# A decoder layer: compressed attention steps moved ahead of the units, and the first layer norm fed tile by tile

## The reference, cut to what matters

```python
h = layer_norm(x, ln_emb_g, ln_emb_b)                    # x: 512 tokens x 1024 features, float32
z = h @ w_in                                             # u, q, three K/V pairs, head gates, mixing gates
y_ssm = s5_branch(u, ...)                                # 32 groups, 64 complex states, scan over tokens, GLU
y_nsa = nsa_branch(q, kv_cmp, kv_slc, kv_win, gates)     # three attentions, each weighted by a gate per head
mixed = (sigmoid(g0) * y_ssm + sigmoid(g1) * y_nsa) @ w_out
h = layer_norm(alpha * h + mixed); h = layer_norm(alpha * h + cross_attention(h, mem))
out = layer_norm(alpha * h + swiglu(h))
...
# the compressed branch of nsa_branch, for each block of queries
s = q @ k_c.T * scale - slope * dist                     # k_c, v_c: 31 compressed keys and values
o_cmp = masked_softmax(s, dist >= 0) @ v_c
```

## Time and profile before

| | |
|---|---|
| median of 3 runs | 1221.28 us |
| the profiled execution | 1217.75 us, span 1216.0 us |
| TensorE busy, mean granted clock | 94%, 0.982 |
| VectorE, ScalarE, GpSimd busy | 44%, 35%, 42% |
| HBM read | 93.59 MB |

### The profile page before, as it was taken

The page is one execution under the profiler, slowest core; times in us unless marked ns, Lnnn a source line. Parts: engine busy times, 40 slices in busy tenths (PEclk is TensorE's granted clock), DMA queues, the critical chain, the costliest instruction groups (busy, mean ns, idle before and its releaser), DMA issues.

```text
span 1216.0 us, 16799 instructions
## 1 busy us (share of the span) xinstructions
PE 1141.4 (94%) x6089; PEld 909.8 (75%) x6089; DVE 540.8 (44%) x1118; ACT 423.6 (35%) x754; POOL 505.4 (42%) x320
## 2 busy tenths in 40 slices
PE   4999989999998989899999899996999999999995
PEld 4988878786885666568887686674888888888884
DVE  8898941220116666765436715366322222210005
ACT  3323315321236656562324614225323223221211
POOL 4652414441143434355555541144544344434442
PEclk9999989999999999999999999998999999999998
DMA  6643313772130000003343431132333333323231
GB/s 167 102 106 83 93 44 91 223 181 60 33 89 18 1 2 1 2 4 119 94 131 112 131 103 35 35 94 78 89 104 90 99 100 89 104 70 104 87 104 69
DMA packets 158383, 101.67 MB, mean 84 GB/s; under 512 B 18344, under 2 KB 145968, under 8 KB 158192
## 3 DMA queue, kind: packets, MB, share of 16 engines
q1 hardware_dynamic: 153408, 94.48, 27.8%
q10 hardware_dynamic: 4912, 6.35, 1.6%
HBM read 93.59 MB, written 2.10 MB: 79 GB/s over the span
## 4 chain that ended last, share of the span: by engine, by line
PE 73%; issue 10%; DVE 8%; POOL 5%; ACT 2%; DMA 1%; POOLq 0%; SPq 0%; DVEq 0%; ACTq 0%
PE bank L1345 70%; POOL wlo L796 5%; PE bank L1625 2%; DVE Sr L1148 2%; DVE xc L862 1%; POOL Sr L833 1%; DVE PTr L1173 1%; DMA xtok<-in_x 1%; PE bank L1403 1%; ACT PTr L673 0%; DVE xtok L889 0%; ACT Sr L663 0%; DVE xPT L1300 0%; DVE Tc L862 0%; DVE st L1325 0%
## 5 line engine op out<-in xcount | busy, mean ns | idle before, releaser
L796 POOL TENSOR_TENSOR wlo<-wraw,whi 128x1024 fp32r<-128x1024 f32 x160 | 394.8, 2469 | 532.2 <-ACT whi L493 532.2
L493 ACT ACTIVATE whi<-wraw 128x1024 fp32r<-128x1024 f32 x160 | 169.3, 1060 | 578.8 <-PE bank L1345 205.8
L1345 PE MATMUL bank<-hHi,whi 128*128 128x512 f32 x736 | 289.5, 393 | 7.9 <-ACT hHi L533 7.8
L1345 PE MATMUL bank<-hHi,wlo 128*128 128x512 f32 x736 | 287.9, 391 | 0.0
L1345 PE MATMUL bank<-hLo,whi 128*128 128x512 f32 x736 | 284.2, 389 | 0.0
L1345 PEld LDWEIGHTS bank<-hHi,whi 128*128 128x128 f32 x736 | 139.1, 189 | 39.4 <-ACT hHi L533 10.0
L1345 PEld LDWEIGHTS bank<-hHi,wlo 128*128 128x128 f32 x736 | 139.1, 189 | 29.1
L1345 PEld LDWEIGHTS bank<-hLo,whi 128*128 128x128 f32 x736 | 138.1, 188 | 28.9 <-POOL hLo L810 0.4
L833 POOL TENSOR_SCALAR Sr<-Sr,winv,gates 128x512 f32<-128x512 f32 (+3 forms) x128 | 77.0, 612 | 101.7 <-DVE winv L1159 101.6
L663 ACT ACTIVATE Sr<-Sr,nmax 128x512 f32<-128x512 f32 (+3 forms) x128 | 71.6, 560 | 67.2 <-DVE nmax L1148 65.6
L862 DVE TENSOR_TENSOR sLo<-sF,sHi 128x512 f32 x22 | 50.0, 2274 | 98.9 <-ACT sHi L738 98.9
(11 more groups left out here) (312 smaller groups left out, 1742.9 us busy)
## 6 DMA issues: line engine op xcount, KB each, us to landing
wraw<-in_ffn_w_in SPq DMA_DIRECT2D x88, 256.0 KB, 3.2
wraw<-in_w_in SPq DMA_DIRECT2D x80, 256.0 KB, 3.4
wraw<-in_ffn_w_out SPq DMA_DIRECT2D x44, 256.0 KB, 2.7
wraw<-in_xattn_w_kv SPq DMA_DIRECT2D x32, 256.0 KB, 3.1
w<-in_cmp_w ACTq DMA_DIRECT2D x1, 4096.0 KB, 19.1
wraw<-in_nsa_w_out SPq DMA_DIRECT2D x16, 256.0 KB, 3.0
wraw<-in_w_out SPq DMA_DIRECT2D x16, 256.0 KB, 3.1
wraw<-in_xattn_w_q SPq DMA_DIRECT2D x16, 256.0 KB, 3.1
```

Source lines behind the costliest of these rows:

```text
L493: act.activation(hi_of(c)[:, :], wraw[c % 4][:, :], ACT.Copy).then_inc(w_hi_ready, 1)
L796: pool.tensor_tensor(wlo[c % 4][:, :], wraw[c % 4][:, :], hi_of(c)[:, :].bitcast(F32), ALU.subtract).then_inc(w_lo_ready, 1)
L1345: return pe.matmul(o, w, a, start=start, stop=stop)
```

## The change

In the front, SP issues `ldt` and `araw` ahead of x. The layer norm goes by token tile: VectorE takes statistics of tile a+1 ahead of scaling tile a, ScalarE takes one square root for each tile; VectorE scales features 0 to 511, ScalarE features 512 to 1023. TensorE turns each token tile when it is ready, with one bank for each of the 8 feature blocks (the eighth waits for the small vectors in bank 7). `split(0)` now stands behind the token work on ScalarE. The u stage starts when four feature blocks are copied; the parameter turns and D stand behind its first 12 matmuls, the C turns behind its first block. In attention, `Tc` has two buffers, `PTc` four, the compressed steps use banks 6 and 7 in turn, and all of them lie among the gmixc tiles. The turns of the units use banks 2, 3 and 7.

```diff
+H0_BANKS, CT_BANKS = (2, 3, 4, 5, 0, 1, 6, 7), (1, 6)
-CMP_SCORE, CMP_EXP, CMP_SUM, CMP_TURN, CMP_COPY = 16, 19, 21, 25, 26
+TURN_BANKS = (2, 3, 7)
...
+            sp_.dma_start(ldt[:, :], ...
+            for i, name in enumerate(("ssm_a_re", "ssm_a_im")):
+                sp_.dma_start(araw[i][:, :, :], ...
             for a in range(4):
                 sp_.dma_start(xtok[:, a, :], I["x"][0, a * P:(a + 1) * P, :]).then_inc(x_landed[a], 16)
...
-            act.wait_ge(var0_ready, 1)
-            act.activation(rinv[:, :], rinv[:, :], ACT.Sqrt).then_inc(sd0_ready, 1)
-            split(0)
             act.wait_ge(par_landed, 48)
             act.activation(araw[2][:, :, :], ldt[:, :, None].to_broadcast([NGP, 2, NS]), ACT.Exp).then_inc(dt_ready, 1)
+            def token_high(a):
+                act.wait_ge(shift0_ready, a + 1)
+                act.activation(xtok[:, a, 512:D], xtok[:, a, 512:D], ACT.Identity, scale=rinv[:, a:a + 1],
+                               bias=shift0[:, a:a + 1]).then_inc(xn_high, 1)
+            for a in range(4):
+                act.wait_ge(var0_ready, a + 1)
+                act.activation(rinv[:, a:a + 1], rinv[:, a:a + 1], ACT.Sqrt).then_inc(sd0_ready, 1)
+                if a >= 1:
+                    token_high(a - 1)
+            token_high(3)
+            split(0)
...
                 act.activation(G[:, GM["gmixc"] + t, :], bank[t % 2][:, :], ACT.Sigmoid).then_inc(tile_act, 1)
+                if t in (3, 5, 6):
+                    compressed_exp({3: 1, 5: 2, 6: 3}[t])
...
+            def token_low(a):
+                dve.wait_ge(sd0_ready, a + 1)
+                link(dve.reciprocal(rinv[:, a:a + 1], rinv[:, a:a + 1]))
+                dve.tensor_scalar(shift0[:, a:a + 1], bnmv[:, a, 0:1], rinv[:, a:a + 1], -1.0, ...
+                dve.tensor_scalar(xtok[:, a, 0:512], xtok[:, a, 0:512], bnmv[:, a, 0:1], rinv[:, a:a + 1],
+                                  ALU.subtract, ALU.mult).then_inc(xn_low, 1)
+            token_stats(0)
+            for a in range(3):
+                token_stats(a + 1)
+                token_low(a)
+            token_low(3)
...
             compressed_scores(0)
             compressed_sums(0)
+            compressed_scores(1)
             compressed_copy(0)
+            compressed_sums(1)
+            compressed_copy(1)
+            compressed_scores(2)
+            compressed_sums(2)
+            compressed_scores(3)
+            compressed_copy(2)
+            compressed_sums(3)
+            compressed_copy(3)
...
+            for a in range(4):
+                if a == 2:
+                    pe.wait_ge(vec_landed, 16 * 12)
...
+                for k in range(7):
+                    pe.wait_ge(xn_low if k < 4 else xn_high, a + 1)
+                    last = turn_token(k, a)
+                    if a == 3:
+                        last.then_inc(h0_turned, 1)
             pe.wait_ge(vec_ready, 1)
+            for a in range(4):
+                last = turn_token(7, a)
+            last.then_inc(h0_turned, 1)
...
-            pe.wait_ge(hf0_ready, KT)
+            pe.wait_ge(hf0_ready, 4)
             for b in range(4):
...
+                    if k == 0:
+                        parameters()
                 last.then_inc(w_used, 1)
+                if b == 0:
+                    turn_c()
...
             compressed_scores(0)
-            for t in range(2, 5):
-                front_tile("gmixc", t)
+            front_tile("gmixc", 2)
+            compressed_scores(1)
+            front_tile("gmixc", 3)
             compressed_turn(0)
-            for t in range(5, 8):
-                front_tile("gmixc", t)
+            front_tile("gmixc", 4)
+            compressed_turn(1)
+            compressed_scores(2)
+            front_tile("gmixc", 5)
+            compressed_scores(3)
+            front_tile("gmixc", 6)
+            compressed_turn(2)
+            front_tile("gmixc", 7)
+            compressed_turn(3)
             pe.wait_ge(tile_act, TA_END)
             pe.wait_ge(ks_landed, 32)
+            pe.wait_ge(ptc_ready, 3)
...
                     pe.wait_ge(scaled, v + 1)
-                    if v >= 2:
-                        pe.wait_ge(turned_act if v % 2 else turned_dve, v // 2)
+                    if v == 2:
+                        pe.wait_ge(ptc_ready, 4)
+                    elif v >= 3:
+                        pe.wait_ge(turned_dve if v % 2 else turned_act, (v - 3) // 2 + 1)
```

More of the change, by code:

```diff
@@ L205, in build @@
     PTr = [at(f"PTr{i}", [P, T], RX + (40 + 2 * i) * KB) for i in range(4)]
-    Tc = at("Tc", [P, NH, 32], RX + 54 * KB)
+    Tc = [at(f"Tc{i}", [P, NH, 32], RX + (52 + 2 * i) * KB) for i in range(2)]
     dist = at("dist", [P, T], RX + 56 * KB)
@@ L210, in build @@
     Vbd = at("Vbd", [P, NKV, 4, HD], RX + 88 * KB)
-    PTc = [at(f"PTc{i}", [P, NKV, P], RX + (94 + 2 * i) * KB) for i in range(2)]
+    PTc = [at(f"PTc{i}", [P, NKV, P], RX + (94, 96, 48, 50)[i] * KB) for i in range(4)]
     mHi = at("mHi", [P, KT, T], RG, F32R)
@@ L874, in _, with token_stats @@
             dve.tensor_copy(rep16[:, :, :], ident[0:GC, None, 0:GC].to_broadcast([GC, 8, GC])).then_inc(rep_ready, 1)
-            for a in range(4):
+            def token_stats(a):
                 dve.wait_ge(x_landed[a], 16)
@@ L965, in _ @@
             dve.memset(sums[:, :, :, :], 0.0)
-            dve.wait_ge(dcol_done, 1)
-            dve.tensor_copy(Dcol[:, :], bank[7][:, 0:NG])
             dve.wait_ge(ct_ready, 2)
@@ L1415, in _, with turn_token @@
-            pe.wait_ge(c_landed, 64)
-            for ri in range(2):
-                for t in range(4):
-                    last = pe.transpose(bank[ri][:, P * t:P * t + P], Craw[:, ri, t, :, :].rearrange("p d n -> p (d n)"),
-                                        ident[:, :])
-                last.then_inc(ct_turned, 1)
-            pe.wait_ge(hf0_ready, KT)
+            def turn_token(k, a):
+                return pe.transpose(bank[H0_BANKS[k]][:, P * a:P * a + P], xtok[:, a, P * k:P * k + P], ident[:, :])
@@ new lines, in _ @@
+            for a in range(4):
+                if a == 2:
+                    pe.wait_ge(vec_landed, 16 * 12)
+                    pe.transpose(bank[7][:, 0:72], vrows[:, :], ident[0:72, 0:72])
+                    pe.transpose(bank[7][0:GC, 128:128 + NG], dl[:, :], ident[0:NG, 0:NG])
+                    for z in range(2):
+                        last = pe.transpose(bank[7][:, 160 + 16 * z:176 + 16 * z], posl[:, z, :], ident[0:16, 0:16])
+                    last.then_inc(vec_turned, 1)
+                for k in range(7):
[3 more added lines that the diff above has]
+                        last.then_inc(h0_turned, 1)
@@ new lines, in _, with parameters @@
+            pe.wait_ge(vec_ready, 1)
+            for a in range(4):
+                last = turn_token(7, a)
+            last.then_inc(h0_turned, 1)
+            def parameters():
+                pe.wait_ge(hf0_ready, 5)
+                pe.wait_ge(rep_ready, 1)
+                mm(bank[0][:, 64:64 + NG], rep16[:, :, :].rearrange("p j c -> p (j c)"), dT[:, :], True, True)
+                pe.wait_ge(par_landed, 48)
+                pe.wait_ge(dt_ready, 1)
+                for i in range(3):
+                    last = pe.transpose(bank[0][:, NGP * i:NGP * i + NGP], araw[i][:, :, :].rearrange("g q n -> g (q n)"),
+                                        ident[0:NGP, 0:NGP])
+                last.then_inc(par_turned, 1)
@@ L1423, in _, with turn_c @@
+            def turn_c():
+                pe.wait_ge(c_landed, 64)
+                pe.wait_ge(hf0_ready, 7)
+                for ri in range(2):
+                    for t in range(4):
+                        last = pe.transpose(bank[CT_BANKS[ri]][:, P * t:P * t + P],
+                                            Craw[:, ri, t, :, :].rearrange("p d n -> p (d n)"), ident[:, :])
+                    last.then_inc(ct_turned, 1)
+            pe.wait_ge(hf0_ready, 4)
             for b in range(4):
```

119 lines of the change are left out of this document (41 added, 78 removed).

## The result

The changed kernel takes 1204.85 us (median of four runs, 1204.12 to 1205.61), against 1221.12 for the kernel before in the same session: a ratio of 0.9856, 95% interval 0.9815 to 0.9896. The forecast was 1210.0 us and a ratio of 0.9908. The time fell inside the range of 1204 to 1217, near its lower end, but the step is 1.4% and not 0.9%, so it lies on the side ("faster by over 1%") to which I gave 0.40, not on the side to which I gave 0.56.

A forecast was written before the change was run, and what follows sets the result against it. TensorE, busy for 94% of the span, was taken as the bound. Attention -10.7 (-16.6 - 1.5 + 7.4) and front -0.5 gave -11.2: 1217.75 to 1206.5 us, on the median 1210.0, range 1204 to 1217.

The forecast's parts named there:

- Steps among the units: Attention: taking the three compressed steps out from among the units saves their waits and slower clock, 16.6 us together.
- steps 2 and 3: Compressed steps among units 48 to 63 and 80 to 95, forecast to cost 5.60 and 5.27 us.
- twins: Groups of 16 units of the same size, one without a compressed step; their time difference was taken as the step's cost.
- step 1: Compressed step among units 16 to 31; with no clean comparison group in the trace, its cost was taken as 5.7 us.
- Third bank: Turns among the units: a wait shrinks by a turn's length at some four places, gaining 1.5 us (ends 0 and 2.9).
- New place: Between gmixc tiles: score groups 5.7, turns 1.1, last wait 1.3 instead of 0.7; attention starts 7.4 us later.
- Rival C: Between gmixc tiles each step's chain over three engines stands open, making the kernel slower: 1231 us, chance 0.04.
- Front: Up to the scan: 1.7 us gained (one in four) or 0.1 (three in four), so 0.5 gained; ends -1.7 and +1.5.
- The clock: Start of the dense block: after TensorE stands for 2 us, a fall to half clock was held likely, three in four.
- my own case for the fast clock: Front without a clock fall: first u block ends at 26.9, parameter chain resumes at 32.0, 1.7 us gained; one in four.
- The slack that I had put to the chain: Before the scan: the first state copy had waited 1.33 us for TensorE, so the parameter chain could be late by that.
- Rival B: The front loses 1.5 us through late x, GpSimd's row and the chain; third bank gives nothing: 1213.6 us, chance 0.18.
- D: Rival: the units' beat isn't TensorE's own, so VectorE or GpSimd takes back half of the 16.6: 1218.4 us, chance 0.08.

The follow-up runs named there:

- two_banks: The changed kernel with the turns of the probabilities in two banks as before, so a turn waits for the copy two units back: 1212.06 us.
- front_only: The kernel before with only the new layer norm, first dense block and that stage's turn banks; attention as before: 1224.26 us, ratio 1.0027.
- memset_late: The changed kernel with GpSimd's clearing of Mst moved from behind the fourth wlo to behind the eighth: 1203.98 us.
- early_m: The changed kernel with parameter turns and er's exp earlier, Mst's clearing later, and the Pw and Cbd products one q tile earlier: 1201.18 us.
- all_three: The changed kernel with parameter turns and er's exp earlier, Mst's clearing later, and ScalarE's first split ahead of the third square root: 1203.48 us.
- params_first: The changed kernel with the parameters' turns ahead of the first dense matmul and the exp for er ahead of the C copies: 1204.66 us.

## Why the prediction was right in part and wrong in part

**Steps among the units: -16.6 forecast, -20.6 measured.** This is the step that failed, by 4.0 us: the mechanism (a step costs its waits and the clock) was right, the price of a step was too low. With the bank below it, the gain of attention was forecast 7.0 us too small. I took the cost of steps 2 and 3 from units 32 to 47 and 64 to 79 as twins. They are longer by what TensorE still works off from the larger units in front: 23.63 - 21.57 = 2.06 and 18.70 - 16.91 = 1.79. The 5.7 for step 1 came out (5.86), but by luck: I had set it a little over the 5.60 of step 2, which was itself 2.06 too low.

**Third bank: -1.5 forecast with ends of 0 and -2.9, -4.5 measured.** A wait that shrinks by about a turn's length is there, but not at four places: 16 turns are held with two banks. The end of 2.9 was drawn from the same too short list (whose four waits sum to 3.2, not 2.9), and about half of the gain is in no list of waits but only in the distances from start to start, so that an end taken from the waits could not hold it.

**New place: +7.4 forecast, +7.7 measured.** Three score groups, three turns and the wait of 1.3 us for the last sums, which came to 1.32. Stepping the three queues through gave the right answer; no other turn waits. Rival C, open steps between the tiles, is refuted.

**Front: -0.5 forecast with ends of -1.7 and +1.5, +2.9 measured (+3.7 between the two profiled executions).** Right were wlo(0) at 17.1 (17.36), the first dense matmul at 20.8 (21.09), and the end of the normalisation at 15.7 to 16.0 (15.87 and 16.26). The clock, for which I had put three in four on a fall, did not fall there in the profiled execution: after 3.17 us without a matmul the dense block goes at 0.235 us a matmul from the second one on, and the windows say 1.00. It is not settled for the kernel by that: two_banks, with the same front, has 3.4 us of half clock, front_only has none, and of all nine profiles with the new layer norm five ran a part of the dense block at half pace, of four with the old one none.

So by my own case for the fast clock the chain should have gone on at 32.0. It went on at 34.1, because

- the C turns, behind which the C copies wait, came at 27.8 and not at 26.9: the dense block began 0.3 later than forecast and holds the parameter turns with a slow restart;
- ScalarE's exp for er stands behind the C copies and needed a table load of its own, 1.28 us at 29.98, and split(2) and the sine's table load stand behind it.

VectorE's wait of 2.04 us for the parameter turns did not hold the chain there, since VectorE then stood idle for 3.51 us until the sine.

And from there it lost 4.6 more, to 5.9, in collisions with GpSimd, of which I had weighed only those up to the angle. The slack that I had put to the chain, the 1.33 us in front of the H copy, was the wrong one: the chain meets TensorE first at Pw. There it had been 4.7 us ahead (77.08 against 81.78), and it was now 5.0 later, so TensorE waited 0.53 us. Its own head start of 2.8 us was gone by then as well: without the wait it would have been there at 81.70. It went in 1.3 us of parameter and C turns (forecast as 1.4), 0.40 for wlo(2), and a slower restart of the matmuls behind each break; the u stage ends only 0.2 us earlier.

The larger part is one for which the forecast had no term, the half clock behind the Pw products (13.7 us for 6.8). From the first of these products to the first H copy it is 16.2 to 16.3 us in the profiles with 6.8 us of half clock, 17.8 to 18.0 with 10.2 and 19.5 with 13.7. So of the 3.7 us, 0.5 is TensorE's later arrival at Pw and 3.2 is the clock; the runs do not settle whether the wait brings it (last section). Rival B had the sign of the front right, and named GpSimd's row and the late chain.

The rule of the Trainium skill, page SBUF — State Buffer, section "Who interferes with whom", was the one to take further. It also says that a VectorE operation with two SBUF inputs is held by a GpSimd operation that reads SBUF but not by one that only writes it, and that a TENSOR_SCALAR can enter a two-port mode and then contends with GpSimd too. The traces agree, though they do not tell an operation's mode. In the changed kernel the clearing of Mst from 39.69 stopped a TENSOR_SCALAR of one SBUF input for 2.6 us, while the TENSOR_TENSOR steps at 39.99 and before it ran in 0.18; in memset_late a two-input product for Pw begun at 65.03 under the clearing (62.90 to 66.0) took its usual 2.28 us, and the one in front of it, begun at 60.63 under a wlo, 4.47.

**Range and chances.** Between the two profiled executions the errors are -4.0 (steps), -3.0 (bank), +0.3 (new place), +4.2 (front), -1.0 between the H copy and gmixc and +0.9 behind the units, neither of which I had counted: -2.6 on a forecast of -11.2. That the time fell inside the range is in part luck, since attention gave 7.0 us more than forecast and the front took 4.2 more, and the two stand against each other; what the 0.9 is was not looked into. The medians lie 16.3 apart, so that 1204.85 is 5.1 under the forecast; half of this is that the profiled execution before was a quick one of its kernel. The bank and the front came out beyond the ends that I had given them. D is refuted: the steps' cost came back in full, and the listed waits of TensorE among the units sum to 3.6 us of 147.1.

## What to carry to other kernels

The cost of a step inside a software pipeline is not the difference to the nearest group of the same size: the lagging stages still work on the sizes in front, and a subtraction holds only between groups with the same history. When an engine is freed earlier, follow the chain that ends at its next wait: here it ran over VectorE, ScalarE's tables and GpSimd. TensorE's head start of 2.8 us was used up by its own breaks in the dense block, and Pw came 0.5 us late on top. A GpSimd operation that moves over a chain of small VectorE steps can cost the chain all that is left of it, and moving one clearing out of the way was worth 4.5 us of that chain. Before a difference of one or two us between two profiles is put down to an edit, the granted clock and the distances from start to start of both must be compared.

## What the runs showed of the hardware that was not expected

**At the start of the dense block** the clock differs between executions of the same code. In the changed kernel it held through 3.17 us without a matmul and beyond; in two_banks, with the same front, it was at half for 3.4 us from 22.0, 1.3 us after the block began and behind a shorter wait (1.90 us). Of the nine profiles with the new layer norm four show such a fall, of 3.4 us or, in early_m, 6.8, and all_three goes at half pace to 27.3. The turns of xtok show the rise: in eight profiles they go 0.21 us apart at first and 0.11 later, with the step between 14.6 and 22.2 us; in the other five they go 0.21 apart to the end. What decides these times stays open.

**Behind the Pw products** the clock fell in all 13 profiled executions, 2 to 5 us after TensorE had begun the products of 32 columns, which follow each other without a gap that the profile shows. There the time at 1.2 of 2.4 GHz was 6.8, 10.2 or 13.7 us. It was 13.7 in five of the seven that waited for Pw (0.53 to 2.07 us) and 10.2 in the other two; of the six that did not wait, four have 10.2 and two 6.8. Each step of 3.4 us costs 1.7 us up to the H copy. This speaks for a longer half clock behind a wait, but the same kernel was not profiled often enough to show it. There is a rival in the same profiles: the two that waited and yet have 10.2 are two_banks and params_first, whose clock had fallen at 22 us already (but so had that of early_m, with 13.7). The cause of the length stays open.
